# Reading the moving operand backwards in every split product of a hybrid attention layer

## The chip, the cores and the metric

The kernel runs on one core of a Trainium2 chip. The metric is device time in microseconds, the median of several executions. The profile shows one further execution, recorded by the hardware profiler.

## What is computed

One layer of a diffusion backbone, for 512 latent tokens and 128 context tokens that share the weights, all in float32:

```python
mod = SiLU(cond) @ w_mod + b_mod            # shift1, scale1, gate1, shift2, scale2, gate2
h   = x * (1 + scale1) + shift1
z   = h @ w_in                              # 2048 -> 3*1024 + 512 + 512 + 64
o   = concat(neighbourhood_attention(z), latent_attention(z)) @ w_o
x   = LayerNorm(alpha * x + gate1 * o)
h   = x * (1 + scale2) + shift2
f   = (silu(h @ w_gate) * (h @ w_up)) @ w_down      # 2048 -> 5632 -> 2048
y   = LayerNorm(alpha * x + gate2 * f)
```

Neighbourhood attention has 8 heads of 128 with a learned relative bias; latent attention has 8 heads, key/value and query rank 512, and a rotary part of 64. The outputs are the two token blocks and the context's keys, values and latent rows.

## The kernel before

All 640 tokens (T; five tiles of P = 128, of which LT = 4 are latent) pass through each stage together. The weights stream once from memory in blocks of 128 x 1024 float32 (`raw`, or `mraw` for the modulation). A product that must keep float32 precision is split: ScalarE writes the upper part of a block in the reduced float32 format (`whi`, `dwh`, `ringh`), VectorE the remainder (`wlo`, `dwl`, `ringl`), activations are split likewise (`hh`/`hl`, `oh`/`ol`, `acth`/`actl`, `fring`), and TensorE adds three products into one PSUM bank: high by high, high by low, low by high. That is the helper `mm3` (L2156 to L2160), its variant `mm3w` (L2633 to L2637) and, written out, the body of the gate/up loop (L2708 to L2710). In each, the first operand of a product is the stationary one (128 x 128, loaded anew for every product) and the second the moving one, whose columns stream past it. The moving operand is 512 weight columns where tokens are the rows of the result (values, latent rows, output projection, down projection), and half of the tokens (HT = 320) or 384 keys where features are (queries, keys, gate and up).

The stages follow one another in the order in which the code is written, with semaphores between the engines: modulation (L2222, L2223, not a split helper), values, eight heads of neighbourhood attention with their query and key projections, latent projections, latent attention (scores by `mla_scores`, L2296 to L2300: `mm3` and two products of the rotary part into the same bank), output projection (`tok_block` over eight row blocks and five banks), the feed-forward's gate and up in a loop over blocks of hidden features (`gu_body`, some 1185 to 2216 us of the profile), the down projection (`down_part`, up to the end). Each group of products into a bank begins with `start=True` and ends with `stop=True`; the last one's increment tells ScalarE or VectorE that they may read the bank, and a wait before the next group tells TensorE that they have read it. The attention's own products with probabilities (`PT`, L2361) and the transposes are plain float32 and go through none of these helpers.

Of the kernel before, what the change touches and what calls it, by code (L numbers as in the profile page):

```python
# [22 lines left out]
HT = T // 2  # L23
# [164 lines left out]
def build(nc, wstream, xT, xtok, cond, bmod, rpb, kcT, vc, ckvcT, krcT, lncol, lnrow, latg, bcol, rope, cap, ident, sel,  # L188
# [14 lines left out]
    with ctx:  # L203
# [76 lines left out]
        qrS = sb("qrS", [P, NH, T], f32r, s2)  # L280
        krS = sb("krS", [P, KEYS], f32r, s2)
        vm = sb("vm", [P, 6, NH * P], f32, s2)
        krl = sb("krl", [P, KEYS], f32r, s2)
# [99 lines left out]
        ps = [ctx.enter_context(nc.psum_tensor(f"ps{i}", [P, 512], f32)) for i in range(8)]  # L383
# [172 lines left out]
        def act_of(u, kk):  # L556

            hi, lo = [x[:, u, kk * HT:(kk + 1) * HT] for x in (acth, actl)]
            return (lo, hi) if 1 <= u < 5 else (hi, lo)
# [1593 lines left out]
        def _(pe):  # L2153
            mm = nc.tensor.matmul

            def mm3(out, ah, al, bh, bl, first, last):  # L2156

                mm(out, ah, bh, start=first, stop=False)  # L2158
                mm(out, ah, bl, start=False, stop=False)  # L2159
                return mm(out, al, bh, start=False, stop=last)  # L2160
# [113 lines left out]
            def stage(i, a, s, na, kcached=None, h=None, only=None):  # L2274
                A = lambda c: at(i, 5, 5 * a + c)
                one = (lambda c: a + c if i is None else i + a + c)

                def scores():
                    if s < 5:
                        bk = 4 if na or s % 2 == 0 else 0  # L2280
                        if s == 0 and na:
                            pe.wait_ge(q_evac, one(1))
                            pe.wait_ge(k_evac, one(1))
                        elif s == 0:
                            pe.wait_ge(kq_lo, 4 * h + 3)
                        elif s == 2 and not na:
                            pe.wait_ge(kq_lo, 4 * h + 4)
                        if not na and s != 1:

                            pe.wait_ge(exp_ready, A(max(s - 1, 0)))  # L2290
                        if s == 0 and i is None and na:

                            pe.wait_ge(o_evac, a)
                        o = slice(s * P, (s + 1) * P)

                        def mla_scores(out, keys):  # L2296

                            mm3(out, qh[:, o], ql_[:, o], kh[:, keys], kl_[:, keys], True, False)
                            mm(out, qrS[:, h, o], krS[:, keys], start=False, stop=False)
                            return mm(out, qrS[:, h, o], krl[:, keys], start=False, stop=True)  # L2300

                        if not na:
                            if s < LT:
                                mla_scores(ps[bk][:, 0:HT], slice(0, HT))
                                mla_scores(ps[bk + 1][:, 0:HT], slice(HT, T)).then_inc(scores_ready, 1)
                            else:
                                mla_scores(ps[4][:, 0:CTX], slice(T, KEYS)).then_inc(scores_ready, 1)
                        elif s < LT:
                            mm(ps[bk][:, 0:NEAR[s]], qT[:, o], kT[:, KEY0[s] * P:KEY1[s] * P], start=True, stop=True)  # L2309
                            mm(ps[bk + 1][:, 0:CTX], qT[:, o], kcached, start=True, stop=True).then_inc(scores_ready, 1)  # L2310
                        else:
                            mm(ps[4][:, 0:CTX], qT[:, o], kT[:, LAT:T], start=True, stop=True).then_inc(scores_ready, 1)

                def transposes():
                    if 2 <= s < 7:
                        t = s - 2
                        pe.wait_ge(p_ready, A(t + 1))
                        if t:
                            pe.wait_ge(pt_free, A(t))
                        elif not na:  # L2320

                            pe.wait_ge(o_evac, a)
                        if t < LT:
                            n = NEAR[t] if na else LAT
                            for k in range(n // P):
                                nc.tensor.transpose(ps[6][:, k * P:(k + 1) * P], pb[:, t % 3, k * P:(k + 1) * P], idt[:, :])  # L2326
                            if na and t == 3:

                                nc.tensor.transpose(ps[5][:, 2 * P:3 * P], kT[:, LAT:T], idt[:, :])
                            last = ps[5][:, P:2 * P] if na else ps[7][:, 0:P]  # L2330
                            nc.tensor.transpose(last, pb[:, t % 3, n:n + CTX], idt[:, :]).then_inc(pt_ready, 1)
                        else:
                            nc.tensor.transpose(ps[6][:, 0:P], pb[:, t % 3, 0:P], idt[:, :]).then_inc(pt_ready, 1)

                if na:
                    if 1 <= s < 6:

                        pe.wait_ge(max_ready, A(s))  # L2340
                    transposes()
                    scores()
                elif only == "turn":
                    transposes()
                elif only == "scores":
                    scores()
                if s == 7:

                    pe.wait_ge(pt_free, A(5))
                    pe.wait_ge(vh_ready, one(1))  # L2350
                    bk = 4 if na else 6
                    if na:
                        mm(ps[bk][:, :], vh[:, LT, :], PT[:, LT, :], start=True, stop=False)
                        for k in (0, 2, 3):
                            mine = [t for t in range(LT) if KEY0[t] <= k < KEY1[t]]
                            q = slice(mine[0] * P, (mine[-1] + 1) * P)
                            mm(ps[bk][:, q], vh[:, k, :], PT[:, k, q], start=False, stop=False)
                        mm(ps[bk][:, :], vh[:, 1, :], PT[:, 1, :], start=False, stop=True)
                    else:
                        for k in range(5):  # L2360
                            mm(ps[bk][:, :], vh[:, k, :], PT[:, k, :], start=(k == 0), stop=(k == 4))  # L2361
                    mm(ps[bk + 1][:, 0:CTX], vh[:, 5, :], PTc[:, :], start=True, stop=True).then_inc(pv_ready, 1)
# [101 lines left out]
            for t in range(TT):  # L2464
                out = ps[4][:, t * P:(t + 1) * P] if t < LT else ps[5][:, 0:P]
# [98 lines left out]
            for b in range(31):  # L2564
# [12 lines left out]
                if b == 30:  # L2577

                    for t, last in ((0, 0), (1, 0), (0, 1), (1, 1), (2, 0), (2, 1), (3, 0), (3, 1), (4, 0), (4, 1)):
                        if t == 0 and last:  # L2580
                            arrived(None, n + 1)
                        o = slice(t * P, (t + 1) * P)
                        for x in range(2):
                            kk, m, w = 12 + 2 * last + x, n + last, slice(x * 512, (x + 1) * 512)
# [12 lines left out]
                if b in WO_ROWS:  # L2597
                    u = WO_ROWS.index(b)
# [33 lines left out]

            def mm3w(out, wh, wl, ah, al, first, last):  # L2633

                mm(out, wh, ah, start=first, stop=False, skip_group_check=True)  # L2635
                mm(out, wh, al, start=False, stop=False, skip_group_check=True)  # L2636
                return mm(out, wl, ah, start=False, stop=last, skip_group_check=True)  # L2637
# [48 lines left out]
            GU_BANK = [0, 2, 3, 1, 2, 0, 3]  # L2686

            def gu_body(i, j):
                for h in range(HALF):
                    u, half = divmod(h, 2)  # L2690
                    s = (HALF * j + h) % 4
                    pe.wait_ge(glo, gu_at(i, j, h + 1))
                    if i is None and j == PLAIN:
                        if h == 0:
                            pe.wait_ge(f_ready, 1)
                        if h in (2, 4, 6, 8):
                            pe.wait_ge(sy_ready, h // 2)
                    elif h == 0:

                        pe.wait_ge(gate0_read, at(i, 2, j - PLAIN))  # L2700
                    out = ps[GU_BANK[u]][:, 0:HT]
                    for k in range(4):
                        w = slice(k * P, (k + 1) * P)
                        kk = 4 * half + k
                        ah, al = act_of(u, kk)
                        first = u < 4 and kk == 0
                        last = u >= 3 and kk == 7
                        mm(out, ringh[:, s, w], ah, start=first, stop=False, skip_group_check=True)  # L2708
                        mm(out, ringh[:, s, w], al, start=False, stop=False, skip_group_check=True)  # L2709
                        ins = mm(out, ringl[:, s, w], ah, start=False, stop=last, skip_group_check=True)  # L2710
                    ins.then_inc(gused, 1)
# [168 lines left out]
```

## Time and profile before

| | |
|---|---|
| median of 3 runs | 2829.41 us (2829.16 to 2832.34) |
| span of the profiled execution | 2831.2 us; the record gives no other time for it |
| TensorE busy | 2786.1 us, 98% |
| VectorE / ScalarE / GpSimd busy | 66% / 36% / 7% |
| mean granted TensorE clock | 0.996 of 2.4 GHz |
| moved by DMA | 379.84 MB, mean 134 GB/s |

Busy time is the union of the intervals that instructions of an engine cover. A matmul's record begins when it begins to stream and its end is modelled, with the pipeline's depth in it; matmuls that follow one another overlap in the records, so the distance between two starts, not the length of one, is what a matmul takes from the engine.

### The profile page before, as it was taken

Reading aid. Unit: us, or ns where it says so; the run is one execution under the profiler, and the core shown is the slowest. Engines: PE = TensorE matmul, PEld = TensorE weight load, DVE = VectorE, ACT = ScalarE, POOL = GpSimd, SP = SyncE. Lnnn points to the kernel's source line nnn. Section 1 sums busy time; section 2 is a strip of 40 time slices with the busy share of each in tenths; the row PEclk is TensorE's granted clock in tenths of the full one; section 3 lists DMA queues with packets and bytes.
Section 4 is the critical chain, followed back from the end, with each engine's and each line's share of the span. In section 5 each row is a group of like instructions: output and inputs, shape, how many; then the busy total and the mean of one; then the engine's idle time right before and its main releaser. Section 6 shows DMA issues by size and latency. Waiting matters only on the chain.

```text
span 2831.2 us, 42083 instructions
## 1 busy us (share of the span) xinstructions
PE 2786.1 (98%) x15881; PEld 2483.6 (88%) x15881; DVE 1879.8 (66%) x2917; ACT 1033.1 (36%) x1804; POOL 186.6 (7%) x260
## 2 busy tenths in 40 slices
PE   8999999999999999999999999999999999999998
PEld 2689999888888778999999999999999888888886
DVE  8766666586895887866666666666666455424338
ACT  7522333234554114544444444444444312112122
POOL 0131111000001000000000000000000000000005
PEclk9999999999999999999999999999999999999999
DMA  9764344362334745222222222222222535224222
GB/s 392 277 197 153 126 132 135 125 198 70 107 119 172 246 154 207 87 96 96 103 99 102 99 91 103 92 98 103 98 103 95 203 123 169 82 84 144 77 104 104
DMA packets 105545, 379.84 MB, mean 134 GB/s; under 512 B 13934, under 2 KB 14226, under 8 KB 103530
## 3 DMA queue, kind: packets, MB, share of 16 engines
q1 hardware_dynamic: 89664, 321.56, 32.7%
q0 software_dynamic: 15488, 56.95, 5.8%
q8 instruction: 63, 1.03, 0.1%
q14 instruction: 32, 0.26, 0.0%
q10 hardware_dynamic: 298, 0.04, 0.0%
HBM read 346.97 MB, written 33.48 MB: 134 GB/s over the span
## 4 chain that ended last, share of the span: by engine, by line
PE 89%; DVE 5%; DMA 3%; ACT 1%; issue 1%; SPq 0%; ACTq 0%; POOLq 0%; DVEq 0%
PE ps L2158 15%; PE ps L2160 15%; PE ps L2159 15%; PE ps L2709 12%; PE ps L2710 12%; PE ps L2708 12%; DMA mraw<-in_wstream 2%; PE ps L2361 1%; PE ps L2326 1%; DMA fst<-fscr 1%; DVE ps L2086 1%; PE ps L2635 1%; PE ps L2637 1%; PE ps L2309 1%; PE ps L2636 1%
## 5 line engine op out<-in xcount | busy, mean ns | idle before, releaser
L2708 PE MATMUL ps<-actl,ringh 128*128 128x320 f32 x1344 | 415.4, 309 | 0.2 <-DVE ringl L1933 0.2
L2709 PE MATMUL ps<-acth,ringh 128*128 128x320 f32 x1344 | 415.3, 309 | 0.0
L2710 PE MATMUL ps<-actl,ringl 128*128 128x320 f32 x1344 | 415.3, 309 | 0.0
L2158 PE MATMUL ps<-dwh,fring 128*128 128x512 f32 x820 | 319.6, 390 | 1.8 <-DVE dwl L2061 1.8
L2160 PE MATMUL ps<-dwh,fring 128*128 128x512 f32 x820 | 319.2, 389 | 0.0
L2159 PE MATMUL ps<-dwl,fring 128*128 128x512 f32 x820 | 319.2, 389 | 0.0
L2708 PE MATMUL ps<-acth,ringh 128*128 128x320 f32 x1008 | 311.5, 309 | 0.0
L2709 PE MATMUL ps<-actl,ringh 128*128 128x320 f32 x1008 | 311.5, 309 | 0.0
L2710 PE MATMUL ps<-acth,ringl 128*128 128x320 f32 x1008 | 311.5, 309 | 0.0
L2061 DVE TENSOR_TENSOR dwl<-raw,dwh 128x1024 fp32r<-128x1024 f32 x82 | 100.4, 1224 | 290.3 <-ACT dwh L1439 290.3
L1933 DVE TENSOR_TENSOR ringl<-raw,ringh 128x512 fp32r<-128x512 f32 x252 | 173.5, 689 | 156.7 <-ACT ringh L1350 156.7
L1512 DVE SCALAR_TENSOR_TENSOR macc<-raw,conds,macc 128x512 f32<-128x512 f32 x390 | 270.8, 750 | 6.1 <-DMA raw<-in_wstream 1.6
L1484 DVE TENSOR_TENSOR wlo<-raw,whi 128x1024 fp32r<-128x1024 f32 x110 | 135.1, 1229 | 209.8 <-ACT whi L990 209.1
L2708 PEld LDWEIGHTS ps<-actl,ringh 128*128 128x128 f32 x1344 | 252.2, 188 | 0.4 <-DVE ringl L1933 0.4
L1350 ACT ACTIVATE ringh<-raw 128x512 fp32r<-128x512 f32 x252 | 159.4, 632 | 255.2 <-PE ps L2710 254.9
L2709 PEld LDWEIGHTS ps<-acth,ringh 128*128 128x128 f32 x1344 | 252.3, 188 | 0.0
L2710 PEld LDWEIGHTS ps<-actl,ringl 128*128 128x128 f32 x1344 | 252.3, 188 | 0.0
L990 ACT ACTIVATE whi<-raw 128x1024 fp32r<-128x1024 f32 x110 | 116.3, 1058 | 370.5 <-PE ps L2160 368.7
L1439 ACT ACTIVATE dwh<-raw 128x1024 fp32r<-128x1024 f32 x82 | 86.9, 1059 | 412.6 <-PE ps L2160 406.3
L2708 PEld LDWEIGHTS ps<-acth,ringh 128*128 128x128 f32 x1008 | 189.2, 188 | 0.0
L2710 PEld LDWEIGHTS ps<-acth,ringl 128*128 128x128 f32 x1008 | 189.2, 188 | 0.0
L2709 PEld LDWEIGHTS ps<-actl,ringh 128*128 128x128 f32 x1008 | 189.2, 188 | 0.0
(364 smaller groups left out, 5913.3 us busy)
## 6 DMA issues: line engine op xcount, KB each, us to landing
raw<-in_wstream SPq DMA_DIRECT2D x503, 512.0 KB, 3.7
mraw<-in_wstream SPq DMA_DIRECT2D x64, 512.0 KB, 7.7
fscr<-fst POOLq DMA_DIRECT2D x44, 320.0 KB, 2.4
fst<-fscr SPq DMA_DIRECT2D x21, 640.0 KB, 4.5
acc<-in_xT SPq DMA_DIRECT2D x8, 640.0 KB, 15.9
oscr<-ost POOLq DMA_DIRECT2D x16, 320.0 KB, 3.5
ostage<-oscr POOLq DMA_DIRECT2D x16, 320.0 KB, 4.0
acc<-in_xtok POOLq DMA_DIRECT2D x4, 1280.0 KB, 9.0
```

What stands on the lines that cost most here:

```text
L990: nc.scalar.activation(hi_of(n), raw[:, slot_of("w", n), :], ACT.Copy).then_inc(hi_ready, 1)
L1350: nc.scalar.activation(ring(ringh, (HALF * j + h) % 4), gu_source(u, half), ACT.Copy).then_inc(ghi, 1)
L1484: V.tensor_tensor(lo_of(n), raw[:, slot_of("w", n), :], hi_of(n).bitcast(f32), ALU.subtract).then_inc(lo_ready, 1)
L1512: ins = V.scalar_tensor_tensor(out=v, in0=w, scalar=f, in1=v, op0=ALU.mult, op1=ALU.add)
L1933: V.tensor_tensor(ring(ringl, s), gu_source(u, half), ring(ringh, s).bitcast(f32), ALU.subtract).then_inc(glo, 1)
L2061: V.tensor_tensor(lo, raw[:, d % 4, :], hi.bitcast(f32), ALU.subtract).then_inc(dlo, 1)
L2158: mm(out, ah, bh, start=first, stop=False)
L2159: mm(out, ah, bl, start=False, stop=False)
L2160: return mm(out, al, bh, start=False, stop=last)
L2708: mm(out, ringh[:, s, w], ah, start=first, stop=False, skip_group_check=True)
L2709: mm(out, ringh[:, s, w], al, start=False, stop=False, skip_group_check=True)
L2710: ins = mm(out, ringl[:, s, w], ah, start=False, stop=last, skip_group_check=True)
```

## The change

Every split product gets its moving operand and its output with the columns in descending order: `[:, ::-1]` is a view that begins at the last element and has a step of minus one. The stationary operand is left as it is. Since operand and output are turned round together, column x of the bank still receives what belongs there, and the instructions that read the bank are unchanged. The two rotary products that accumulate into the bank of the latent scores are turned round as well. No instruction is added, removed or moved, on any engine.

```diff
@@ -2155,6 +2155,7 @@
 
             def mm3(out, ah, al, bh, bl, first, last):
 
+                out, bh, bl = out[:, ::-1], bh[:, ::-1], bl[:, ::-1]
                 mm(out, ah, bh, start=first, stop=False)
                 mm(out, ah, bl, start=False, stop=False)
                 return mm(out, al, bh, start=False, stop=last)
@@ -2296,8 +2297,9 @@
                         def mla_scores(out, keys):
 
                             mm3(out, qh[:, o], ql_[:, o], kh[:, keys], kl_[:, keys], True, False)
-                            mm(out, qrS[:, h, o], krS[:, keys], start=False, stop=False)
-                            return mm(out, qrS[:, h, o], krl[:, keys], start=False, stop=True)
+                            back = out[:, ::-1]
+                            mm(back, qrS[:, h, o], krS[:, keys][:, ::-1], start=False, stop=False)
+                            return mm(back, qrS[:, h, o], krl[:, keys][:, ::-1], start=False, stop=True)
 
                         if not na:
                             if s < LT:
@@ -2632,6 +2634,7 @@
 
             def mm3w(out, wh, wl, ah, al, first, last):
 
+                out, ah, al = out[:, ::-1], ah[:, ::-1], al[:, ::-1]
                 mm(out, wh, ah, start=first, stop=False, skip_group_check=True)
                 mm(out, wh, al, start=False, stop=False, skip_group_check=True)
                 return mm(out, wl, ah, start=False, stop=last, skip_group_check=True)
@@ -2698,11 +2701,11 @@
                     elif h == 0:
 
                         pe.wait_ge(gate0_read, at(i, 2, j - PLAIN))
-                    out = ps[GU_BANK[u]][:, 0:HT]
+                    out = ps[GU_BANK[u]][:, 0:HT][:, ::-1]
                     for k in range(4):
                         w = slice(k * P, (k + 1) * P)
                         kk = 4 * half + k
-                        ah, al = act_of(u, kk)
+                        ah, al = [x[:, ::-1] for x in act_of(u, kk)]
                         first = u < 4 and kk == 0
                         last = u >= 3 and kk == 7
                         mm(out, ringh[:, s, w], ah, start=first, stop=False, skip_group_check=True)
```

## Rows read from the trace of the kernel before

**Rows 1.** The page: span, busy time of each engine, forty slices.

```profile
span 2831.2 us, 42083 instructions
...
PE 2786.1 (98%) x15881; PEld 2483.6 (88%) x15881; DVE 1879.8 (66%) x2917; ACT 1033.1 (36%) x1804; POOL 186.6 (7%) x260
...
PE   8999999999999999999999999999999999999998
```

**Rows 2.** Stretches: length, busy us (instructions) by engine, granted clock, DMA share, GB/s.

```profile
1300.00:1500.00 200.00, 200.00 (x1366) 200.00 (x1365) 136.39 (x204) 85.50 (x155) 4.32 (x8) 1.00 0.27 97
2300.00:2800.00 500.00, 500.00 (x2206) 412.82 (x2205) 225.54 (x268) 102.65 (x95) 18.10 (x9) 1.00 0.32 108
```

**Rows 3.** Who waited for whom: us in total, times, longest.

```profile
ACT ringh L1350 <- PE ps L2710: 585.5, 580, 1.4
...
PE ps L2222 <- DVE mlo L1535: 14.3, 34, 7.3
```

**Rows 4.** Timeline of TensorE in the gate/up stage: start us, length us.

```profile
1499.75 0.31 PE L2708 MATMUL ps<-acth,ringh 128*128 128x320 f32 x1
...
1503.86 0.31 PE L2709 MATMUL ps<-actl,ringh 128*128 128x320 f32 x1
```

**Rows 5.** Timeline of TensorE in the down stage.

```profile
2599.64 0.39 PE L2158 MATMUL ps<-dwh,fring 128*128 128x512 f32 x1
...
2603.95 0.39 PE L2159 MATMUL ps<-dwl,fring 128*128 128x512 f32 x1
```

**Rows 6.** Groups by line and shape, TensorE: count, busy us, mean ns, idle before.

```profile
L2708 PE MATMUL ps<-actl,ringh 128*128 128x320 f32 x1344 | 415.4, 309 | 0.2 <-DVE ringl L1933 0.2
...
L2158 PE MATMUL ps<-dwh,fring 128*128 128x512 f32 x820 | 319.6, 390 | 1.8 <-DVE dwl L2061 1.8
...
L2708 PE MATMUL ps<-acth,ringh 128*128 128x320 f32 x1008 | 311.5, 309 | 0.0
...
L2158 PE MATMUL ps<-hh,whi 128*128 128x320 f32 x512 | 162.8, 318 | 0.9 <-ACT qT L1108 0.9
...
L2158 PE MATMUL ps<-whi,hh 128*128 128x512 f32 x320 | 125.9, 393 | 0.0
L2158 PE MATMUL ps<-whi,oh 128*128 128x512 f32 x320 | 125.6, 393 | 1.0 <-DVE ol L1794 0.6 <-DVE wlo L1484 0.4
...
L2361 PE MATMUL ps<-PT,vh 128*128 128x512 f32 x70 | 31.2, 592 | 0.0
L2158 PE MATMUL ps<-fring 128*128 128x512 f32 x60 | 23.3, 389 | 0.0
...
L2158 PE MATMUL ps<-kh,qh 128*128 128x320 f32 x64 | 22.6, 353 | 1.2 <-ACT pb L1089 1.2
L2158 PE MATMUL ps<-ckvh,whi 128*128 128x384 f32 x64 | 22.0, 344 | 0.0
...
L2158 PE MATMUL ps<-qlh,whi 128*128 128x320 f32 x64 | 20.2, 315 | 0.7 <-issue 0.7
...
L2300 PE MATMUL ps<-krl,qrS 128*128 128x320 f32 x64 | 19.9, 312 | 0.0
...
L2635 PE MATMUL ps<-acth,ringh 128*128 128x320 f32 x64 | 19.8, 309 | 0.0
...
L2158 PE MATMUL ps<-whi,ckvh 128*128 128x512 f32 x48 | 19.2, 401 | 0.0
...
L2635 PE MATMUL ps<-acth 128*128 128x320 f32 x48 | 16.7, 348 | 0.9 <-DVE actl L1892 0.9
...
L2158 PE MATMUL ps<-whi,qlh 128*128 128x512 f32 x20 | 7.9, 394 | 0.0
...
L2635 PE MATMUL ps<-acth,early 128*128 128x320 f32 x16 | 5.6, 349 | 1.0 <-DVE actl L1892 1.0
```

**Rows 7.** The chain that ended last, 731 to 738 us: start us, length us.

```profile
731.45 0.15 PE ps L2300
731.60 4.29 PE ps L2361 x10
```

## Prediction

> **What bounds the kernel now.** I read the page first. TensorE is busy in 2786.1 of the span's 2831.2 us and sits at 9 tenths in almost every slice, while VectorE is busy for 66% and ScalarE for 36% of it [rows 1]. The view of stretches shows the same from inside [rows 2]: from 1300 to 1500 us and from 2300 to 2800 us TensorE is busy in every microsecond at a granted clock of 1.00 (2.4 GHz), VectorE in 136 of 200 and 226 of 500, and DMA moves about a third of what its engines have time for. The list of TensorE's own waits has fifteen rows, from 14.3 us (the modulation's L2222, which is not changed [rows 3]) down to 0.2 us (at the end of the first row of [rows 6]), some 32 us together. ScalarE waits 585.5 us for TensorE to release a gate/up buffer [rows 3]; that is the slack of an engine that runs ahead and costs nothing. So the time is the sum of the starts of TensorE's products, one behind the other, and the question is only how far apart they start.
>
> The busy times in the grouped view cannot tell that: a product of 320 columns is shown with 309 ns and one of 512 with 389 ns, but these overlap, since the end is modelled. The starts tell it. In the timeline 28 distances between products of 320 columns take 1503.86 - 1499.75 = 4.11 us, 0.147 us each [rows 4], and 19 between products of 512 columns 2603.95 - 2599.64 = 4.31 us, 0.227 us each [rows 5]. The stretches give it more finely: 1366 products in 200 us are 146.4 ns each (all of 320 columns), 2206 in 500 us are 226.7 ns each (all of 512) [rows 2]. The difference, 80.3 ns for 192 columns, is 0.418 ns a column, one tick of 2.4 GHz. What is left over is 146.4 - 320 x 0.4167 = 13.1 ns and 226.7 - 512 x 0.4167 = 13.4 ns, a fixed part of each product. I carry two prices then: 0.417 ns for each column, 13.2 ns for each product.
>
> **How much of the kernel the change touches.** From the grouped view [rows 6]; each row stands for the three lines of one split product, which have equal counts. Of 320 columns: 1344 + 1008 + 512 + 64 (scores) + 64 (queries) + 128 (L2635: 64 + 48 + 16) = 3120, times 3 = 9360, and 128 of L2299 and L2300, the rotary part of the scores: 9488. Of 512 columns: 820 + 60 + 320 + 320 + 48 + 20 = 1588, times 3 = 4764. Of 384 columns: 64 x 3 = 192. Some forty of 128 columns are left out. That is 14,444 of 15,881 products, and they take 9488 x 146.4 + 4764 x 226.7 + 192 x 173 ns = 1389 + 1080 + 33 = 2502 us, 88% of the span. Nothing hides them: whatever a reversed product costs more or less than a forward one falls on the end almost one to one.
>
> **The change part by part.** Removed and added: nothing. Every matmul, its weights, its wait and its increment stay, in the same order. What differs is inside the instruction: the moving operand starts at its last element with a step of minus one, and so does the output. Each product pairs column x of the operand with column x of the bank as before, all products of one accumulation agree, and the readers of a bank wait for the last product of its group, so no engine sees a different moment at which data is there. The modulation products (L2222, L2223), the transposes and the float32 products stay forward. The DMAs, ScalarE and VectorE get the same work. The weights, which each product loads anew (as many loads as matmuls on the page, 15881 each [rows 1]), are read forward as before.
>
> So the sum has one unknown, the price of a column and of a start when the step is -1. No row of this trace has a negative step on TensorE, so I bound it from the rows that are nearest.
>
> Nearest of all is the forward product itself [rows 4, 5]: same element width, same banks, same number of elements, each next to the one before. By it the change is worth 0, and the time stays at the median of 2829.4 us (the profiled execution shows a span of 2831.2 us, 1.8 more than that median and inside the three runs' 2829.16 to 2832.34, so I add nothing between the two).
>
> On the far side lies what a product costs when it does not get one column each tick. The float32 products of attention are such a row: their width is 512 columns (L2361 in [rows 6]), and ten of them take 4.29 us in the chain of work [rows 7], 429 ns each or 0.838 ns a column, twice the split product's price, from the same memories. If a reversed stream fell to that pace, 512 columns would cost 429 in place of 226.7 ns, 320 would cost 268 in place of 146.4, and 384 322 in place of 173: 4764 x 202.3 + 9488 x 121.7 + 192 x 149 ns = 964 + 1155 + 29 = 2147 us more. This end is 2829 + 2147 = 4976 us. Were the fixed 13.2 ns kept on top, it would be 14,444 x 13.2 ns = 191 us more, 5167 us.
>
> Between the ends, what decides is whether the reads and writes are slowed by the order of neighbours or only by their distance. With a step of -1 two consecutive elements are still neighbours in memory. The first one of a bank is column 511, 383 or 319, always the upper one of an aligned pair (also of an aligned four), so a pair (511, 510) is the same pair as (510, 511). The distance is thus as in the forward rows; only a mechanism that looks for a step of exactly +1 would tell them apart. I take the forward row, 0.417 ns and 13.2 ns.
>
> One rule speaks against it. The Trainium skill, "PSUM — Partial Sum Buffer", Specifications, gives PSUM cachelines of 8 bytes and says that "any non-contiguous AP slows matmuls significantly"; "Advanced Engine Details and Errata", Memory Cachelines, explains it as every two consecutive elements having to be contiguous, and asks for two hits on a 16-byte line in SBUF. Read by its letter for lines, a step of -1 passes both (two hits on each PSUM line, four on each SBUF line) and the sum stays at 2829; read as "step of +1 or nothing", it is the slow end above. No row here has a strided product, so the trace doesn't say which. The forward rows, one column per tick with all neighbours in place, agree with both readings.
>
> **The rivals.**
>
> *A reversed stream is served one element where two are served now* (slower, 4976 us). The place is either the operand's read or the bank's accumulating write; it decides at once, because there is no slack on TensorE [rows 2]. The stricter reading of the Trainium skill's "PSUM — Partial Sum Buffer", Specifications, is this rival. For it, from the rows: a column at 0.417 ns of four bytes is twice the pace of the float32 row [rows 7], so something pairs or speeds these accesses, and what pairs may want ascending order. Against it: float32 products are slower for the arithmetic's sake as likely as for the memory's, and pairing by line, not by direction, is all that is needed here.
>
> *The column price stays and the fixed part grows* (slower). A reversed start could cost some ticks: each further nanosecond per product is 14,444 x 1 ns = 14.4 us, or 0.5%. With 1 ns the time is 2844, with 5 ns 2902, with the fixed part doubled 3020 us. For it: there is a fixed part of 13.2 ns whose origin the trace does not show. Against it: it is equal for 320 and 512 columns and for operands at any offset (the scores' operands start at column 0 or 320 and such a product takes 0.15 us, the gate/up pace, in the chain of work [rows 7]), so it doesn't look like a matter of addresses.
>
> *The fixed part shrinks* (faster). If the 13.2 ns came from a product that begins to accumulate at column 0 while the one before still writes the end of the bank, another order could change it; gone altogether it gives 2829 - 191 = 2638 us, and VectorE, with 136 of 200 us busy, would keep up. But in the reversed order too each product begins where its predecessor began and ends where that ended, so the distance between the two writes of one column is the same. Only at the few places where a forward product meets a reversed one does it differ.
>
> *The change does nothing that can be seen* because direction is free is my forecast; that the step would be turned back to +1 on the way to the chip I hold for unlikely, and its time would be the same.
>
> **How the numbers follow.** No change: 0.75, since it asks only that neighbours count as neighbours in either order. Half pace: 0.17. A fixed cost of some ns: 0.05, most of it under 5 ns. The fixed part smaller: 0.03. The predicted time is that of the first, 2829.4 us. A difference of 0.2%, 5.7 us or 0.4 ns per product, is about what a measurement of this kernel can tell from no change. The likeliest case's own range is 2824 to 2835. The range of eight in ten adds the case of a fixed cost up to 5 ns (2902, taken as 2905) and about 1 ns of gain (2815), and leaves out the half pace and what is beyond. Faster 0.03, same 0.75 less a little for noise and for a tick or so per product, slower 0.17 + 0.05 and that little.
>
> **What the changed kernel's profile would show.** If I am right: 1366 and 2206 products within a few in the same two stretches, starts 0.146 and 0.227 us apart, a granted clock of 1.00 there, VectorE's share unchanged, and a span of 2831. If the stream runs at half pace: starts about 0.27 and 0.43 us apart, a span near 5000, VectorE near 40%, and L2222 and the transposes as before; which of the two, read or write, that view could not tell. If only a start costs more: the difference of the two distances stays 80 ns and both grow by the same amount. What would make the prediction wrong is above all an access path that knows only ascending order; second, a clock that falls below 1.00 in those stretches, for which I see no cause, as the engine stays as busy as it was.

## The result: one per cent slower, and the profile after

The changed kernel took 2861.27 us (median of four runs) where the kernel before took 2830.66 us (median of four); the ratio is 1.0103, with a 95% interval of 1.009 to 1.0117. One of the four runs took 8187.73 us and is left out of the ratio. The loss is 29 us by the ratio and 30.6 us by the two medians. Sixty-four products of 320 columns that are written out apart from the helpers (L2424 and L2425 of the kernel before) stay forward, so "every split product" is short by these; they play no part in what follows.

The page, its span and the busy time of each engine:

```profile
span 2859.6 us, 42083 instructions
...
PE 2815.4 (98%) x15881; PEld 2486.0 (87%) x15881; DVE 1879.2 (66%) x2917; ACT 1032.9 (36%) x1804; POOL 186.1 (7%) x260
```

TensorE's busy time grew by 29.3 us (from 2786.1, [rows 1]) and the span by 28.4; VectorE's and ScalarE's did not move. What TensorE does not fill is 44 us, where it was 45. So no wait took anything: the products themselves got dearer. The two stretches say which (columns as in [rows 2]):

```profile
1300.00:1500.00 200.00, 200.00 (x1366) 200.00 (x1365) 136.48 (x204) 85.12 (x155) 4.88 (x9) 1.00 0.27 97
2300.00:2800.00 500.00, 500.00 (x2145) 402.85 (x2144) 205.23 (x233) 100.05 (x93) 4.37 (x6) 1.00 0.33 111
```

From 1300 to 1500 us there are 1366 products, the same number as before: 146.4 ns each, 320 columns. From 2300 to 2800 us there are 2145 where there were 2206: 233.1 ns each in place of 226.7. The granted clock is 1.00 in both. The groups by line and shape (to be held against [rows 6]; the helpers' lines moved by one, the gate/up ones by three):

```profile
L2711 PE MATMUL ps<-actl,ringh 128*128 128x320 f32 x1344 | 418.1, 311 | 0.2 <-DVE ringl L1933 0.2
...
L2159 PE MATMUL ps<-dwh,fring 128*128 128x512 f32 x820 | 326.0, 398 | 0.6 <-DVE dwl L2061 0.6
...
L2159 PE MATMUL ps<-ckvh,whi 128*128 128x384 f32 x64 | 22.5, 352 | 0.0
```

The modelled length of a 512-column product went from 390 to 398 ns (`dwh,fring`), that of 384 columns (`ckvh,whi`) from 344 to 352, that of 320 columns from 309 to 311, though the starts of the 320-column products are no further apart. The timeline of the down stage, for the starts themselves:

```profile
2599.74 0.40 PE L2161 MATMUL ps<-dwh,fring 128*128 128x512 f32 x1
...
2603.93 0.40 PE L2161 MATMUL ps<-dwh,fring 128*128 128x512 f32 x1
```

Eighteen distances make 4.19 us, 0.233 us each, against 0.227 in [rows 5]. 4764 products of 512 columns by 6.4 ns are 30.5 us, a little more than the whole loss.

### The profile page after: what moved, and what is told of

It is laid out like the page before. It is cut to its first block, busy times and chain, and to the rows that moved or that the text cites. A ratio compares the mean times of both kernels' runs of the same rounds, so it can differ in the third digit from the quotient of the medians.

```text
span 2859.6 us, 42083 instructions
## 1 busy us (share of the span) xinstructions
PE 2815.4 (98%) x15881; PEld 2486.0 (87%) x15881; DVE 1879.2 (66%) x2917; ACT 1032.9 (36%) x1804; POOL 186.1 (7%) x260
## 4 chain that ended last, share of the span: by engine, by line
PE 93%; DVE 3%; DMA 2%; ACT 1%; issue 1%; SPq 0%; ACTq 0%; DVEq 0%
PE ps L2159 16%; PE ps L2160 16%; PE ps L2161 16%; PE ps L2711 12%; PE ps L2713 12%; PE ps L2712 12%; DMA mraw<-in_wstream 2%; PE ps L2363 1%; PE ps L2328 1%; PE ps L2638 1%; PE ps L2640 1%; PE ps L2639 1%; PE ps L2311 1%; PE ps L2359 0%; DVE mlo L1535 0%
## 5 line engine op out<-in xcount | busy, mean ns | idle before, releaser
L2159 PE MATMUL ps<-dwh,fring 128*128 128x512 f32 x820 | 326.0, 398 | 0.6 <-DVE dwl L2061 0.6
L2160 PE MATMUL ps<-dwl,fring 128*128 128x512 f32 x820 | 325.8, 397 | 0.0
L2161 PE MATMUL ps<-dwh,fring 128*128 128x512 f32 x820 | 325.8, 397 | 0.0
```

## The experiments

### Which side costs: the read or the write

Only one of the two is turned round, so the columns of each result lie in reverse order and the amount of work stays. `e1_read_back`, in `mm3` (and likewise in the other three places):

```diff
-                out, bh, bl = out[:, ::-1], bh[:, ::-1], bl[:, ::-1]
+                bh, bl = bh[:, ::-1], bl[:, ::-1]
```

> Only the moving operand is read backwards; every split product writes its bank forwards, so that the columns of each result lie in reverse order (the output is not the reference's; the amount of work is). In the changed kernel the products of 512 columns start 233.1 ns apart where they were 226.7, those of 320 columns 146.6 as before. Theory A (the descending write into the bank is the cost): this kernel is at the time of before, 2830 us, and its 512-column products start 226.7 ns apart. Theory B (the descending read is the cost): 2860 us and 233.1 ns. Theory C (both directions together, or the mere fact of a negative step anywhere, in the decoding of the instruction): also 2860, and then the kernel with only the write turned round is at 2860 too.

`e2_write_back`:

```diff
-                out, bh, bl = out[:, ::-1], bh[:, ::-1], bl[:, ::-1]
+                out = out[:, ::-1]
```

> Only the bank is written backwards; the moving operand is read forwards, so that the columns of each result lie in reverse order (the output is not the reference's; the amount of work is). Theory A (the descending write is the cost): 2860 us, 512-column products 233.1 ns apart. Theory B (the descending read): 2830 us and 226.7 ns. Theory C: 2860 here as well as with only the read turned round. If each direction costs a part, the two kernels' increases add up to about 30 us.

With only the read backwards: 2859.99 us, ratio 1.0103 (1.0086 to 1.012). With only the write backwards: 2830.31 us, ratio 0.9999 (0.999 to 1.0009). The stretches, first with the read backwards (gate/up and down), then with the write (down):

```profile
1300.00:1500.00 200.00, 200.00 (x1366) 200.00 (x1365) 136.51 (x204) 85.73 (x155) 4.86 (x9) 1.00 0.27 99
2300.00:2700.00 400.00, 400.00 (x1716) 322.33 (x1715) 160.36 (x182) 76.25 (x71) 3.25 (x4) 1.00 0.33 111
```

```profile
2300.00:2700.00 400.00, 400.00 (x1765) 330.30 (x1764) 169.32 (x192) 79.07 (x73) 4.36 (x6) 1.00 0.33 113
```

1716 products in 400 us are 233.1 ns, 1765 are 226.6. The whole cost is the read's; a bank written from its last column to its first costs nothing that the whole kernel's time shows. Theory B held, A and C fell.

### Which products cost: the wide ones

`e4_wide_back` reverses, read and write, only what is wider than 320 columns; `e3_narrow_back` only the rest. All wide products go through `mm3`; the other three places are as before in `e4_wide_back` and as in the changed kernel in `e3_narrow_back`, whose condition in `mm3` is `<= HT`.

```diff
+                if out.shape[-1] > HT:
+                    out, bh, bl = out[:, ::-1], bh[:, ::-1], bl[:, ::-1]
```

> Only products of more than 320 columns are turned round (512 and 384), read and write both; the gate/up products and all others of 320 columns and less are as before. By the starts in the changed kernel's trace the whole loss lies in the 512-column products: 4764 x 6.4 ns = 30 us. So 2860 us, the changed kernel's time. The rival, that the loss is a cost per product of any width of which the 320-column ones hide their part in the stretches looked at but not elsewhere (about 1 to 2 ns on each of 14,444 products), gives 2830 + 4956 x 2 = 2840 us.

> The half of the change that the wide one left out: products of 320 columns and fewer are turned round (gate/up through its own lines, queries, keys, scores), those of 384 and 512 are as before. 9,488 products. Standing alone a row of 320 columns took 146.6 ns forward and 146.7 backward. If the narrow products are free in the kernel too: 2830 us, ratio 1.000. If reversal costs them something where other engines read and write at the same time (1 ns each): 2840 us.

Wide: 2858.26 us, ratio 1.0099 (1.0083 to 1.0116). Narrow: 2831.9 us, ratio 1.0006 (0.9997 to 1.0016), which is no change. The down stage of the narrow one is at the old pace, 400 us / 1764 = 226.8 ns:

```profile
2300.00:2700.00 400.00, 400.00 (x1764) 330.22 (x1763) 168.79 (x192) 79.24 (x74) 4.37 (x6) 1.00 0.34 113
```

So 4956 of the 14,444 reversed products make the loss, and 9488 pay nothing that can be measured: the upper end of the interval, 0.16% or 4.5 us, leaves room for 0.5 ns on each.

### The read with nothing else running

`e5_widths_alone` is the kernel of before with rows of 64 products added ahead of the value projection, one line of code per row, `wk` and `wv` being columns 512 to 639 and 0 to 511 of a block of weights, for example

```diff
+            for x in range(64): mm(ps[5][:, 0:384], wk, wv[:, 0:384][:, ::-1], start=False, stop=True, skip_group_check=True)
```

> The kernel of before with 35 rows of 64 split-format products each added ahead of the value projection, all with the same weights and operand, into a bank that is not in use; the other engines stand still meanwhile. Read here is only the distance between starts. Theory W (a descending stream costs some ticks for each column, and narrow products hide it because another limit applies to them): forward distance = 0.4167 N + 13.3 ns, reversed grows with N, with nothing at 320, 6.4 ns at 512 and something between at 352, 384 and 448. Theory X (the descending reads of 512 columns lose against ScalarE's and VectorE's writes into the same block of weights): no difference between forward and reversed here, at any width. Theory Y (a step at the full bank): 6.4 ns at 512 and 0 at 448. The rows with reading or writing alone tell which side costs; if the order of pairs or 16-byte lines matters, blocks of 2 or 4 in descending order cost the full amount, if the order within a line matters only the row with lines ascending and their elements descending does. Alternating direction: if a new product has to stay behind the last one's write of the same column, these rows are slower by much; if the fixed 13.3 ns came from that, the rows with two banks are faster than 226.7 ns. A read with a step of two, 256 columns: 120 ns if free, 220 if half the pace is lost.

The timeline merges each row of 64 into one line: start us, length us, line. The distance between the starts of two neighbouring lines, divided by 64, is the price of one product of the first. From L2262 to L2271 the second line of each width reads and writes backward.

```profile
158.99 9.55 PE L2262 MATMUL ps<-whi 128*128 128x320 f32 x64
168.37 9.55 PE L2263 MATMUL ps<-whi 128*128 128x320 f32 x64
177.76 10.48 PE L2264 MATMUL ps<-whi 128*128 128x352 f32 x64
...
198.46 11.29 PE L2266 MATMUL ps<-whi 128*128 128x384 f32 x64
209.59 11.54 PE L2267 MATMUL ps<-whi 128*128 128x384 f32 x64
220.96 13.13 PE L2268 MATMUL ps<-whi 128*128 128x448 f32 x64
...
247.15 14.70 PE L2270 MATMUL ps<-whi 128*128 128x512 f32 x64
261.69 15.10 PE L2271 MATMUL ps<-whi 128*128 128x512 f32 x64
276.62 9.55 PE L2272 MATMUL ps<-whi 128*128 128x320 f32 x64
...
317.87 15.09 PE L2276 MATMUL ps<-whi 128*128 128x512 f32 x64
332.80 14.69 PE L2277 MATMUL ps<-whi 128*128 128x512 f32 x64
347.33 9.76 PE L2278 MATMUL ps<-whi 128*128 128x320 f32 x64
356.93 15.10 PE L2279 MATMUL ps<-whi 128*128 128x512 f32 x64
371.86 14.71 PE L2280 MATMUL ps<-whi 128*128 128x512 f32 x64
...
401.35 14.69 PE L2282 MATMUL ps<-whi 128*128 128x512 f32 x64
415.88 15.10 PE L2283 MATMUL ps<-whi 128*128 128x512 f32 x64
...
490.15 14.67 PE L2288 MATMUL ps<-whi 128*128 128x512 f32 x64
504.66 14.88 PE L2289 MATMUL ps<-whi 128*128 128x256 f32 x64
519.36 14.70 PE L2290 MATMUL ps<-whi 128*128 128x512 f32 x64
```

L2262 and L2263 are 320 columns forward and backward: 9.38 and 9.39 us, 146.6 and 146.7 ns. L2266 and L2267, 384 columns: 11.13 and 11.37 us, 173.9 and 177.7 ns. L2270 and L2271, 512 columns: 14.54 and 14.93 us, 227.2 and 233.3 ns. This is what the kernel shows, with VectorE and ScalarE running no instruction and a granted clock of 1.00 (columns as in [rows 2]), so Theory X (contention with their writes) fell:

```profile
155.00:530.00 375.00, 375.00 (x1875) 331.47 (x1874) 0.00 (x0) 0.00 (x0) 0.00 (x0) 1.00 0.00 1
```

At 448 columns the difference was 3.9 ns, so Theory Y (a step at the full bank) fell as well. Theory W (a cost that grows with the width above 320 columns) got something at 352, 384 and 448, as it asked: 0.9, 3.8 and 3.9 ns; the finer widths below show that it does not grow steadily. L2276 reads backward and writes forward (14.93 us), L2277 the other way round (14.53): the read again.

Three more things stand in these lines. L2282 and L2283 use two banks in turn, forward and backward, and cost 227.0 and 233.4 ns (the line after the second is not shown), the same as one bank: neither the reversal's cost nor the fixed 13.3 ns comes from one product following another into the same bank. L2279 alternates direction, of read and write together, from one product to the next and costs 14.93 us, 233.3 ns, as if all were backward; at 320 columns alternating (L2278, 9.60 us, 150.0 ns) costs 3.4 ns where neither direction alone costs anything. And L2288, in which each group of four columns is reversed but the groups ascend, costs 226.7 ns, nothing, while L2289, 256 columns with a step of two, costs 229.7 ns where 256 columns in a row cost 120.3 (not shown).

### The same three orders in the whole kernel

The helper function that turns an operand is replaced. Blocks of 64 columns, the last block first, ascending within (`e6_blocks64`); blocks of 16 (`e7_blocks16`); groups of four reversed, the groups ascending (`e8_in_line`):

```diff
-                out, bh, bl = out[:, ::-1], bh[:, ::-1], bl[:, ::-1]
+                out, bh, bl = turned_(out), turned_(bh), turned_(bl)
...
+                return x.rearrange("p (n q) -> p n q", q=64)[:, ::-1, :]
```

> Every split product of the changed kernel takes its columns, on the read and the write side, in blocks of 64 (256 bytes) from the last block to the first, ascending within a block. Standing alone, such a stream of 512 columns had no cost (14.53 us for 64 products, 227.0 ns each, where full reversal took 233.3). Theory G (what costs is going down from one piece of 64 to 128 bytes to the next; seven steps between 256-byte blocks are too few to cost): time of before, 2830 us, 512-column products 226.7 ns apart. The rival, that any operand whose last column comes first costs (the address of the start), gives 2860 us.

> The same with blocks of 16 columns (64 bytes), last block first, ascending within. Standing alone it cost as much as full reversal (233.3 ns). Theory G: 2860 us and 233.1 ns in the 512-column products, 146.6 ns in the 320-column ones. If the negative step of the innermost direction were what costs in the kernel, its time would be that of before, 2830 us.

> Each group of four columns (16 bytes) is read and written from its last to its first, but the groups come in ascending order: a negative innermost step in every split product. Standing alone it cost nothing (226.7 to 227.0 ns). Theory G: time of before, 2830 us. If the negative step itself, or a pattern of two dimensions, costs in the kernel: 2860 us.

Blocks of 64: 2830.61 us, ratio 0.9999 (0.999 to 1.0009). Blocks of 16: 2860.51 us, 1.0105 (1.0088 to 1.0122). Groups of four: 2830.0 us, 0.9999 (0.9989 to 1.0009). The down stage of the three, in this order:

```profile
2300.00:2700.00 400.00, 400.00 (x1765) 330.20 (x1764) 169.12 (x192) 79.05 (x73) 4.37 (x6) 1.00 0.34 113
```

```profile
2300.00:2700.00 400.00, 400.00 (x1716) 322.28 (x1715) 160.44 (x182) 75.52 (x70) 3.25 (x4) 1.00 0.34 112
```

```profile
2300.00:2700.00 400.00, 400.00 (x1764) 330.17 (x1763) 168.10 (x191) 79.88 (x74) 4.36 (x6) 1.00 0.34 114
```

226.6, 233.1 and 226.8 ns. A negative step inside groups of four columns costs nothing (the third), and neither does going backward through the operand in pieces of 256 bytes (the first). Going backward in pieces of 64 bytes, though ascending within each, costs as much as full reversal. All three expectations by Theory G (what costs is going down from one piece of 64 to 128 bytes to the next) held; `e10_groups_offsets` below speaks against it.

### How large the piece is, and finer widths

`e9_widths_finer`, more rows of the same kind, all written forward.

> Again rows of 64 products each ahead of the value projection with the other engines still; the write is forward in all. Thirteen more widths from 264 to 504, read forward and backward. Theory Q: the distance between starts comes in slots of 6.67 ns (16 ticks of 2.4 GHz): it was 120.3, 146.6, 173.9, 227.0 ns forward at 256, 320, 384 and 512 columns, 22 slots at 320 and 34 at 512, and 35 reversed (233.3); widths between give mixtures of two neighbouring slots. Then a small cost per descending step pushes a product into the next slot at 512 and not at 320. By Theory Q 288 columns take 133.3 ns, 416 take 186.7, 480 take 213.3 forward, and the reversed read adds either 0 or up to 6.7 ns, never more. Rival P: the cost is proportional to the width above some 340 columns, without steps. Blocks of 8, 32, 64, 128, 256 columns descending: by Theory G 8 costs 6.3 ns, 64 and up nothing, 32 (128 bytes) tells the size of the piece. A stationary operand of 4 columns in place of 128: if the descending read loses against the weight load of the next product, 512 columns then take the same forward and backward; if not, 6.3 ns remain. The same with the weights at another place of the same tile: no change expected.

Blocks of 32, 64 and 128 columns in descending order (L2283 to L2285; the line after L2285 is not shown), then the operand forward and backward with the weights at another place of the tile (L2291, L2292):

```profile
424.51 15.10 PE L2283 MATMUL ps<-whi 128*128 128x512 f32 x64
439.44 14.68 PE L2284 MATMUL ps<-whi 128*128 128x512 f32 x64
453.97 14.67 PE L2285 MATMUL ps<-whi 128*128 128x512 f32 x64
...
531.40 14.69 PE L2291 MATMUL ps<-whi 128*128 128x512 f32 x64
545.93 15.10 PE L2292 MATMUL ps<-whi 128*128 128x512 f32 x64
560.87 15.10 PE L2293 MATMUL ps<-whi 128*128 128x512 f32 x64
```

L2283 costs 14.93 us, 233.3 ns; L2284 14.53 us, 227.0; L2285 226.6. For descending blocks the border lies between 128 and 256 bytes. With other weights 227.0 and 233.4 ns remain. With four stationary columns in place of 128 the two directions took 231.1 and 233.4 ns: the backward read reaches the same 233.4, which speaks against a lost race with the next product's weight load; but 2.3 ns remain where the expectation had either 0 or 6.3, since the forward price moved by 4 ns for a reason I didn't find. At 320 columns the four stationary columns made a small cost of reversal appear: 145.3 ns forward and 146.7 backward.

The widths, in ns for one product, worked out from the starts as above:

| columns | 264 | 272 | 288 | 304 | 336 | 368 | 400 | 416 | 432 | 464 | 480 | 496 | 504 |
|---|---|---|---|---|---|---|---|---|---|---|---|---|---|
| forward | 120.0 | 125.3 | 131.9 | 137.8 | 153.3 | 166.9 | 180.2 | 186.9 | 195.8 | 209.1 | 216.7 | 223.4 | 227.0 |
| backward | 120.0 | 124.5 | 133.3 | 140.2 | 153.3 | 166.9 | 182.3 | 191.1 | 197.5 | 211.2 | 219.8 | 226.7 | 228.9 |

Theory Q (slots of 6.67 ns) asked for 213.3 at 480 and 133.3 at 288 and fell: they are 216.7 and 131.9. (It allowed mixtures of two neighbouring slots, so a value between two slots, such as 209.1, does not speak against it by itself.) Rival P (in proportion above 340) fell too: 0 at 368, 4.2 at 416, 1.7 at 432. At 272 columns, and at 256 (`e5_widths_alone`: 120.3 forward, 118.4 backward), the backward order was even the cheaper one. What the table does show is that forward 512 columns are a favourable case: 504 columns cost as much as 512 (227.0), and from 432 to 504 the part beyond 0.4167 ns a column is 15.8 to 17.0 ns, where at 512 it is 13.7.

### Groups and starting places

`e10_groups_offsets`, rows again: groups of g columns reversed inside, groups ascending; and operands that begin at another column.

> Rows of 64 products as before, written forward, other engines still. In groups of g columns that are reversed inside and follow one another in ascending order: if what costs is each descent across a 128-byte boundary, then groups of 4 to 32 columns cost nothing, 64 (8 descents within, and jumps upward between) half or less, 128 and 256 nearly all of the 6.3 ns at 512 columns. If it is the longest unbroken run downward that counts, 64 and 128 stay free and 256 costs. If any descent over 64 bytes counts, 32 costs already (it has one inside each group). Blocks of 32 and 64 in descending order at 320 and 384 columns: at 384 the 32-blocks cost 3.8 ns as full reversal did and the 64-blocks nothing; at 320 neither costs. Offsets of the operand's first column (0 to 128) and of the weights: if the cost comes from where the stream stands against some boundary of 256 bytes or more, it changes with the offset, and forward streams change too; if it is a cost of direction alone, 3.8 ns at 384 and 6.3 ns at 512 remain at each offset.

Groups of 4, 8, 16 and 32 at 512 columns (L2256 to L2259):

```profile
117.72 14.67 PE L2256 MATMUL ps<-whi 128*128 128x512 f32 x64
132.23 15.08 PE L2257 MATMUL ps<-whi 128*128 128x512 f32 x64
147.15 17.23 PE L2258 MATMUL ps<-whi 128*128 128x512 f32 x64
164.21 15.52 PE L2259 MATMUL ps<-whi 128*128 128x512 f32 x64
179.57 15.09 PE L2260 MATMUL ps<-whi 128*128 128x512 f32 x64
```

226.7, 233.1, 266.6 and 240.0 ns; groups of 64, 128 and 256 gave 233.3 to 233.4. None of the readings that I had written down asks for this, and Theory G falls with them: groups of 8 never go down by more than 32 bytes and still cost 6.4 ns: the dearest order is not the one with the longest way down but the one that reverses 64 bytes at a time. And forward streams paid for their starting place: 512 columns from column 16 cost 228.9, from 32 232.3, from 64 227.0 again. At 384 columns a start at 32 or 96 cost 175.9 against 173.4, and the backward read cost 0.8 to 4.4 ns more than the forward one from the same start. Blocks of 32 columns in descending order cost 2.5 ns there in place of the 3.8 expected, blocks of 64 nothing, and at 320 columns neither cost anything. Four other places of the weights left the backward price of 512 columns at 233.3 to 233.4.

The last two kernels took this up. `e12_groups16` is `e8_in_line` with groups of 16 in all split products; `e11_groups_narrow` has rows at 320 columns and more starting places.

```diff
-                return x.rearrange("p (n q) -> p n q", q=4)[:, :, ::-1]
+                return x.rearrange("p (n q) -> p n q", q=16)[:, :, ::-1]
```

> Every split product reads and writes its columns in groups of 16 that are reversed inside, the groups in ascending order: the same rows of memory as before, never more than 15 columns downward. Standing alone, 512 columns read so took 266.6 ns where ascending took 226.7. If what stands alone holds in the kernel, the 4764 products of 512 columns alone add 4764 x 39.9 = 190 us: at least 3020 us; with 320 columns hit in proportion (25 ns on 9488 products, 237 us) 3257 us. Theory D (the cost of a descending read is a price for each step down past a 16-byte line): full reversal has 127 such steps and this has 96, so it would cost less than full reversal, under 2860 us. The measurement that stands alone already speaks against D; the kernel shows what it is worth in the whole.

> Rows of 64 products standing alone. At 320 and 384 columns, groups of 4, 8, 16, 32, 64 columns reversed inside: if 320 columns are exempt from any cost of order, all five are at 146.7; if they are exempt only because full reversal happens to fit, groups of 16 cost them some 25 ns, in proportion to 512 columns' 40. Offsets of the first column: forward streams of 512 columns were 227.0, 228.9, 232.3, 227.0 ns at 0, 16, 32, 64. If only the place within a piece of 64 columns (256 bytes) counts, 40 and 24 lie beside 32, 8 and 56 beside 0, and 320 columns show the same pattern. Blocks of 64 in descending order cost nothing from column 0; if their freedom comes from starting at a multiple of 256 bytes, the same blocks moved by 32 columns cost 5 ns or more; if any such block is free, they stay at 227.0.

The whole kernel with groups of 16: 3201.57 us, ratio 1.1309 (1.129 to 1.1328), 13% slower for an order that never goes down by more than 15 columns. Its stretches, gate/up and down:

```profile
1300.00:1500.00 200.00, 200.00 (x1202) 200.00 (x1202) 126.09 (x179) 78.06 (x135) 4.55 (x8) 1.00 0.26 89
2700.00:3000.00 300.00, 300.00 (x1127) 216.00 (x1126) 99.47 (x110) 49.74 (x46) 0.00 (x0) 1.00 0.26 85
```

200 us / 1202 = 166.4 ns at 320 columns, 300 us / 1127 = 266.2 ns at 512. 9488 x 20.0 + 4764 x 39.5 ns = 190 + 188 = 378 us; measured were 371. The expectation's 25 ns for 320 columns was 5 too many, and with it its 3257 us. Theory D (a price for each step down past 16 bytes) fell by 340 us. Standing alone, at 320 columns groups of 16, then of 32 (L2258, L2259), and at 512 columns forward streams that begin at column 0, 8 and 64 (L2276, L2277, L2284), and blocks of 64 in descending order from column 32 and from column 0 (L2290, L2291):

```profile
134.82 10.83 PE L2258 MATMUL ps<-whi 128*128 128x320 f32 x64
145.48 9.97 PE L2259 MATMUL ps<-whi 128*128 128x320 f32 x64
155.29 9.55 PE L2260 MATMUL ps<-whi 128*128 128x320 f32 x64
...
316.76 14.69 PE L2276 MATMUL ps<-whi 128*128 128x512 f32 x64
331.28 15.10 PE L2277 MATMUL ps<-whi 128*128 128x512 f32 x64
346.22 14.82 PE L2278 MATMUL ps<-whi 128*128 128x512 f32 x64
...
435.60 14.69 PE L2284 MATMUL ps<-whi 128*128 128x512 f32 x64
450.13 15.10 PE L2285 MATMUL ps<-whi 128*128 128x512 f32 x64
...
525.00 15.03 PE L2290 MATMUL ps<-whi 128*128 128x512 f32 x64
539.88 14.72 PE L2291 MATMUL ps<-whi 128*128 128x512 f32 x64
554.43 17.23 PE L2292 MATMUL ps<-whi 128*128 128x512 f32 x64
```

At 320 columns: 166.6 and 153.3 ns, so these products are not exempt from a cost of order; but groups of 4, 8 and 64, full reversal, and every start from 0 to 64 in either direction, took 146.6 to 146.9. At 512: 226.9 from column 0, 233.4 from column 8, 227.0 from 64; of those not shown 233.4 from 32; from 24, 48 and 56 it was 233.3 to 233.4, from 40 234.2 and from 16 again 228.9. The blocks of 64 cost 232.5 ns when moved by 32 columns and 227.3 when not. So a forward stream of 512 columns that does not begin at a multiple of 256 bytes costs nearly what the backward one does (column 16 excepted). From columns 8, 24 and 48 direction made no difference at all: 233.3 to 233.4 ns either way; from 32 the backward read took 236.6 (236.7 in `e10_groups_offsets`, where the forward one took 232.3). Columns are counted in the tile here; where the tile itself lies in memory was not varied.

## Why the prediction failed

**What bounds the kernel** was right and carried the whole reading: no slack, 98% TensorE, cost one to one. The sum by it comes out: with the prices that the runs showed, 4764 x 6.4 + 192 x 4 ns = 31 us; 29 were measured.

**The step that failed** is "I take the forward row, 0.417 ns and 13.2 ns", on the ground that neighbours stay neighbours and pairs and fours stay the same. For the write this was right (0.9999), and for order inside four columns too (0.9999). But the read of 512 columns also depends on how the stream lies on pieces of 256 bytes, which I did not consider at all: 226.7 ns is the price of a stream that begins on such a border and ascends, at least within pieces of that size, and about 233 of most others. The prediction said that only a mechanism that looks for a step of exactly +1 would tell the two apart; the runs with blocks of 64 and groups of four, both with a negative step and both free, show that it was not that either. Nor was the "fixed part of each product" fixed: it was read from 320 and 512 columns, where it is 13.1 and 13.4 ns, but at 448 columns it is 16.0 (202.7 ns).

**The rivals.** Half pace did not happen: nothing like 0.838 ns a column, 4976 us was far off. The Trainium skill's rule on PSUM ("PSUM — Partial Sum Buffer", Specifications: "any non-contiguous AP slows matmuls significantly") does not reach to descending order; with the write alone reversed the time stayed. A growing fixed part was the nearest rival, and at its stated price of 14.4 us for each further nanosecond the loss is 2.0 ns as a mean over all reversed products; but its mark, that both distances grow equally and their difference stays 80 ns, is refuted: 320 columns grew by 0 and 512 by 6.4 ns, and the difference is now 86.7. Against it I had argued that the fixed part was equal for operands at any offset; the offsets that I looked at, 0 and 320 columns, are both multiples of 64, and the products 320 wide, which are exempt; and the row that I cited is a single product, read to 10 ns. This argument compared only cases that could not differ. The fixed part's disappearance did not happen, and two banks in turn showed that it isn't the accumulation's.

**The numbers.** 2861 lies inside the range of 2815 to 2905, but by luck: the range reached there for a fixed cost on every product, given 0.05, which is not what happened. No change had 0.75, and the loss of 1.0% is beyond the 0.2% that the prediction took for no change. The mis-sized term is the price of reading 512 columns backward, given as 0 and measured as 6.4 ns.

**What stays open.** Why 320 columns (and 264, 336 and 368) are exempt from reversal, and 320 from a shifted start, though not from groups of 16; why 256 and 272 gain a little by it; why groups of 16 are the worst; and what is kept in pieces of 256 bytes. The weight load's place and width were varied without moving the backward price, the bank and the other engines are excluded; beyond that the cause is not settled. A whole kernel that reads forward from a shifted column was not tried, so that the starting place costs the same in the kernel as in the rows that stand alone is likely by the other agreements but not shown.

## What to carry to other kernels

On a kernel that TensorE fills, the order in which the moving operand is read is a term of its own, and what counts is the order and the starting place at 32 to 256 bytes, not the sign of the step: 512 columns of four bytes should ascend from a multiple of 64 columns. (Measured for split products that each load their own weights.) Reverse the output if something needs to be reversed: the write was free. And before you argue from rows that two cases cost the same, look whether those rows could have differed at all; here a few rows of 64 products, put into the program where the other engines stood still, gave prices that add up to 4764 x 39.9 + 9488 x 20.0 ns = 380 us for the kernel with groups of 16, which lost 371.

## What the runs showed of the hardware

- A split product with its weight load, read forward, takes 13.3 to 17.0 ns beyond 0.4167 ns a column from 320 to 512 columns; at 128 and 192 columns it takes 110.8 and 112.2 ns, so going from 192 to 128 columns saved next to nothing.
- Writing a bank in descending order costs nothing (2830.31 us, ratio 0.9999). Groups of four columns reversed, on both sides, cost nothing (2830.0 us, ratio 0.9999).
- Reading 512 columns: 226.7 to 227.3 ns ascending from a multiple of 64 columns, 228.9 to 234.2 from elsewhere, 233.1 to 233.4 backward (236.6 and 236.7 from column 32), 240.0 and 266.6 ns in groups of 32 and 16 reversed inside.
- A read with a step of two costs 229.7 ns for 256 columns, against 120.3 without: half the pace. The Trainium skill ("Advanced Engine Details and Errata", Memory Cachelines) asks for two hits on a 16-byte line to hide the access; here there are two on each, and it isn't enough.
- Turning the direction of read and write from one product to the next costs 3.4 ns at 320 columns, where neither direction costs anything.
